# A streaming encoder layer on one Trainium2 core: first level of the triangular inverse by transposes, gate products placed elsewhere in the mixer

## What is computed

```
glu, qkv, b_raw, a_raw, z, gates = jnp.split(xn @ w_in, pts, axis=-1)
c_in = glu[..., :CONV_DIM] * jax.nn.sigmoid(glu[..., CONV_DIM:])
c, conv_new = causal_dwconv(c_in, conv_prev, conv_dw_w)          # 31 taps
c = jax.nn.silu(layer_norm(c + conv_dw_b, conv_ln_g, conv_ln_b))
qkv, dconv_new = causal_dwconv(qkv, dconv_prev, dn_conv_w)       # 4 taps, then silu
...
a_mat = jnp.where(strict, beta[..., :, None] * kk * decay, 0.0) + jnp.eye(chunk)
sol = lax.linalg.triangular_solve(a_mat, rhs, left_side=True, lower=True)
...
delta = u_c - jnp.einsum('bhck,bhkv->bhcv', w_c, s)
o = jnp.einsum('bhck,bhkv->bhcv', qg_c, s) + jnp.einsum('bhij,bhjv->bhiv', qk_c, delta)
s = gl_c[..., None, None] * s + jnp.einsum('bhck,bhcv->bhkv', kd_c, delta)
...
o = o * lax.rsqrt(jnp.mean(o * o, -1, keepdims=True) + EPS) * dn_norm_g
o = o * jax.nn.silu(z)
```

## Time and profile before

| | us |
|---|---|
| three runs | 4794.46, 4795.47, 4798.47 (median 4795.47) |
| span of the profiled execution | 4798.7 |
| projections, 61.6 to 656 | 594.4 |
| layer norm, 656 to 804.4 | 148.4 |
| four prompt tiles, 804.4 to 1375 | 570.6 |
| streams, 1375 to 1566.5 | 191.5 |
| merge, output projection, queries, to 2337 | 770.5 |
| experts, to the end | 2461.7 |

### The profile page before, as it was taken

One profiled execution on the slowest core, in us unless ns is written; L12 is line 12 of the kernel. 1 busy time (PEld: TensorE's weight loads), 2 busy tenths in 40 slices (PEclk: granted clock), 3 DMA queues, 4 the chain that ended last, 5 costly groups with the idle time before them and its releaser, 6 DMA issues. The chain is left out here.

```text
span 4798.7 us, 84568 instructions
## 1 busy us (share of the span) xinstructions
PE 4555.8 (95%) x28205; PEld 4362.4 (91%) x28205; DVE 3410.1 (71%) x4571; ACT 1318.1 (27%) x2054; POOL 1324.8 (28%) x936
## 2 busy tenths in 40 slices
PE   8999989999999999999688999999999999999995
PEld 8999989999998998999678999999999999999994
DVE  4889882334433331068896898888899999999998
ACT  4232323222221221142372222222222222222222
POOL 0111132121212333323002333333333333333333
PEclk8999999999999999999899999999999999999998
DMA  3222323221224433232268999999999999999998
GB/s 119 83 87 87 88 66 98 72 69 60 73 76 154 136 113 144 72 121 70 75 201 330 366 362 365 368 361 367 368 370 381 378 378 375 376 376 374 381 377 332
DMA packets 283687, 1085.62 MB, mean 226 GB/s; under 512 B 23696, under 2 KB 104464, under 8 KB 209936
## 3 DMA queue, kind: packets, MB, share of 16 engines
q0 software_dynamic: 74752, 538.99, 28.6%
q1 hardware_dynamic: 168336, 400.91, 25.3%
q10 hardware_dynamic: 40320, 142.10, 7.6%
HBM read 1017.03 MB, written 64.88 MB: 225 GB/s over the span
## 5 line engine op out<-in xcount | busy, mean ns | idle before, releaser
L489 PE MATMUL ps<-xhi,hi 128*128 128x320 f32 x2560 | 775.4, 316 | 32.2 <-POOL lo L1391 15.6
L489 PE MATMUL ps<-xlo,hi 128*128 128x320 f32 x2560 | 763.7, 311 | 0.0
L2460 PE MATMUL ps<-xhi,whi 128*128 128x384 f32 x2048 | 693.9, 339 | 18.0 <-issue 18.0
L2499 PE MATMUL ps<-ahi,vhi 128*128 128x384 f32 x1536 | 667.5, 435 | 33.8 <-DVE workr L2737 33.8
L2460 PE MATMUL ps<-xlo,whi 128*128 128x384 f32 x2048 | 689.9, 337 | 0.0
L2573 ACT ACTIVATE whi<-work 128x1024 fp32r<-128x1024 f32 x240 | 254.6, 1061 | 1522.3 <-PE ps L2465 1437.3
L2799 DVE CUSTOM_DVE_ANT_0 work<-work,keep 128x2048 f32<-128x2048 f32 x256 | 585.0, 2285 | 35.3 <-DMA work<-in_peer_u,cur_u 23.9
L2764 DVE SCALAR_TENSOR_TENSOR keep<-work,act_w,keep 128x2048 f32<-128x2048 f32 x256 | 600.2, 2345 | 1.9 <-DVE keep L2826 0.9
L2863 POOL DMA_INDIRECT work<-in_peer_v,cur_v x256 | 371.4, 1451 | 754.7 <-DVE keep L2764 729.4
L489 PEld LDWEIGHTS ps<-xhi,hi 128*128 128x128 f32 x2560 | 486.5, 190 | 37.3 <-POOL lo L1391 16.2
L2500 PE MATMUL ps<-alo,vhi 128*128 128x384 f32 x1536 | 520.1, 339 | 0.0
(11 more groups left out here) (336 smaller groups left out, 8186.9 us busy)
## 6 DMA issues: line engine op xcount, KB each, us to landing
work<-in_v_units ACTq DMA_DIRECT2D x256, 512.0 KB, 8.1
work<-in_u_units SPq DMA_DIRECT2D x240, 512.0 KB, 8.0
keep<-in_w_first SPq DMA_DIRECT2D x160, 512.0 KB, 3.6
keep<-in_w_units SPq DMA_DIRECT2D x32, 1024.0 KB, 4.9
gates_dram<-work SPq DMA_DIRECT2D x8, 3072.0 KB, 11.8
gbuf<-gates_dram SPq DMA_DIRECT2D x31, 768.0 KB, 9.6
arena<-in_w_units SPq DMA_DIRECT2D x32, 512.0 KB, 4.0
gates_T<-keep SPq DMA_DIRECT2D x32, 320.0 KB, 2.2
```

The costliest lines, as they stand in the source:

```text
L489: m = pe.matmul(out[:, o:o + HT], w[:, k, :], x[:, 8 * kh + k, c], start=kh == 0 and i == 0, stop=kh == 1 and i == 23)
L2460: pe.matmul(out, h3[:, k, :], (xlo if m % 2 else xhi)[:, 8 * half + k, :], start=half == 0 and m == 0, stop=False)
L2499: pe.matmul(out, vh, a_h, start=False, stop=False)
```

## The change

1. **First level of the inverse.** T starts as the identity, so the first level's products with T are replaced: T's transpose becomes identity minus the masked A (VectorE alone), and T becomes identity minus the transpose of that, which TensorE makes by eight transposes. The identity copies (L1281, L1282), ScalarE's `xc(0)` and the 16 products at L619 and L622 of level 0 go; VectorE writes the mask of level 1 in the same six steps.
2. **Gate filler.** 384 gate matmuls ahead of the layer norm's sums, 228 behind its loop (312 and 300 before). `high` of half 82 moves ahead of the last two spills of q and k on ScalarE, and s and hi steps move among the squares. In a tile 24 follow the new first level (34 in the old), and the tile ends with 58, the output transposes, 30 (before 78, the transposes). In the streams there are 34 ahead of the first head's update, and 72 at the end.
3. **Waits of the projections.** q waits for the sigmoid of the pass before (`evac["gate"]`, whose first count ScalarE gives behind the small chain on `a_log`, L758), and k for `glu_done`.
4. **Streams.** `spread(0)` goes ahead of the output sum, `decay(0)` ahead of the root; the output transposes and last multiply follow head 2.
5. **End.** SP no longer waits for `gate_st` at the end of the mixer; the two places of the next block that need it do.

```diff
-            prompt = {2 * 4: 2 * LEVELS, 2 * 4 - 2: 2 * LEVELS - 2, 2 * 4 + 1: 2 * LEVELS + 1, 4 * 4 - 2: 4 * LEVELS - 2}.get(per, per)
+            prompt = {2 * 4: 2 * LEVELS, 2 * 4 - 2: 2 * LEVELS - 2, 4 * 4 - 6: 4 * LEVELS - 6}.get(per, per)
...
             late_store(7)
             sp.wait_ge(next_ld, 32)
-            sp.wait_ge(gate_st, 16 * 2 * KD)
             sp.wait_ge(out_done, 32)
...
                     if kd == "q":
+                        pe.wait_ge(evac["gate"], c + 1)
+                    elif kd == "k":
                         pe.wait_ge(glu_done, c + 1)
...
-            gates(312)
+            gates(384)
...
-            gates(300)
+            gates(228)
...
                 gates(30)
-                for l in range(lev):
+                w(dd["at"], tot(2, 2))
+                for g in range(2):
+                    w(dd["atl"], tot(2 * lev, g + 1))
+                    for h in range(4 * g, 4 * g + 4):
+                        m = pe.transpose(ps[1][:, h * P:(h + 1) * P], atl[:, h, :], ident)
+                    m.then_inc(dd["x"], 1)
+                gates(24)
+                for l in range(1, lev):
...
-                    gates(78)
+                    gates(58)
+                    out_rows()
+                    gates(30)
                 else:
                     for h in range(H):
-                        gates(32)
+                        gates(34 if h == 0 else 32)
...
+                        if h == 2:
+                            out_rows()
+                    gates(72)
...
             act.sem_inc(norm_root["q"], 1)
+            act.sem_inc(evac["gate"], 1)
...
                 if more:
                     high(c * 10 + 15, 15, wait)
+                else:
+                    high(NPROJ + 2, NPROJ + 2, wait)
                 for kd in "qk":
                     wait(norm_done[kd], c + 2)
                     spill(c, kd)
...
-                    xc(0)
                     s(1, 0)
                     s(1, 1)
                     xc(1)
...
-                lk(v.tensor_copy(tb, bm(ident)))
-                v.tensor_copy(ttb, bm(ident)).then_inc(dd["tt"], 1)
...
+                for g in range(2):
+                    hs = slice(4 * g, 4 * g + 4)
+                    w(dd["atl"], tot(2 * lev, g + 1))
+                    v.tensor_tensor(ttb[:, hs, :], bm(ident, 4), atl[:, hs, :], ALU.subtract).then_inc(dd["tt"], 1)
+                    w(dd["x"], tot(2 * lev, g + 1))
+                    v.tensor_tensor(tb[:, hs, :], bm(ident, 4), ps8(1)[:, hs, :], ALU.subtract).then_inc(dd["t"], 1)
+                    w(dd["tt"], tot(2 * lev, g + 1))
+                    v.tensor_tensor(atl[:, hs, :], atb[:, hs, :], bm(cst[:, LEV0 + 1, :], 4), ALU.mult).then_inc(dd["atl"], 1)
...
             sp.wait_ge(mg_out, 1)
+            sp.wait_ge(gate_st, 16 * 2 * KD)
             gates(1)
...
             merge_weight(1, 1, None)
+            act.wait_ge(gate_st, 16 * 2 * KD)
             split(ohi, of, 3, o_hi)
```

More of the change, by code:

```diff
@@ L291, in build @@
         s1_ld, s2_ld = [sem(f"s1_ld{i}") for i in range(3)], [sem(f"s2_ld{i}") for i in range(5)]
-        gate_mm, gate_act, gate_st = sem("gate_mm"), sem("gate_act"), sem("gate_st")
+        gate_mm, gate_act = sem("gate_mm"), sem("gate_act")
+        gate_st = ctx.enter_context(nc.semaphore("gate_st"))
         gate_out = at(CT + 4096, T)
@@ L406, in _ @@
             next_raw(N0 + 7)
-            sp.wait_ge(dd["tx"], count_s(14, 14))
+            sp.wait_ge(dd["tx"], count_s(10, 10))
             state_1(1)
@@ L541, in gate_steps @@
                 return steps, pos
-            pe.wait_ge(evac["gate"], NC)
+            pe.wait_ge(evac["gate"], NC + 1)
             gates, done = gate_steps(0, NPROJ, NPROJ, lambda s, v: pe.wait_ge(s, v))
-            gates(312)
+            gates(384)
             pe.wait_ge(cconv_out, NC)
@@ L568, in delta, with out_rows @@
                 lev = 4 if streams else LEVELS
+                def out_rows():
+                    w(dd["oscaled"], tot(1, 1))
+                    for h in range(H):
+                        m = pe.transpose(ps[2][:, h * P:(h + 1) * P], xb[:, h, :], ident)
+                    m.then_inc(dd["otr"], 1)
                 gates(0 if streams else 38)
@@ L869, in _ @@
             hi(7)
+            s(3, 0)
+            hi(8)
+            s(3, 1)
+            hi(9)
             for kd in "qkv":
@@ L884, in _ @@
             square(1)
-            s(3, 0)
+            hi(10)
             square(2)
+            s(4, 0)
             square(3)
-            s(3, 1)
-            hi(9)
             square(4)
+            s(4, 1)
+            hi(11)
             square(5)
             square(6)
-            hi(10)
             square(7)
-            s(4, 0)
             act.wait_ge(ln_sqmm, NC)
             act.activation(at(LMEAN, T), ps[2][:, 0:T], ACT.Sqrt, bias=epsc[:, 0:1], scale=1.0 / CONV).then_inc(ln_root, 1)
-            s(4, 1)
-            hi(11)
             hi(12)
+            s(5, 0)
+            s(5, 1)
+            hi(13)
             act.wait_ge(ln_scaled, 1)
@@ L1188, in iteration @@
                 wait(unit_done, c * 10 + 10)
-                wait(evac["gate"], c + 1)
+                wait(evac["gate"], c + 2)
                 wait(prefix_done["c"], c * 16 + 16)
@@ L1323, in delta, with spread, decay, out_rows @@
                 v.tensor_tensor(vc, vc, tb, ALU.subtract).then_inc(dd["r2"], 1)
+                bmask = cst[:, BLK_S, :]
+                def spread(h):
+                    v.tensor_tensor(at(SLOT[3 if h % 2 else 6], NB, P), atl[:, h, :].unsqueeze(1).to_broadcast([P, NB, P]),
+                                    bmask[:, NT - 1::NT].unsqueeze(2).to_broadcast([P, NB, P]), ALU.mult).then_inc(dd["dm"], 1)
+                def decay(h):
+                    st_h = at(S2[h % 5], NB, P)
+                    glb = smalld[:, 64 + NB * h:64 + NB * h + NB].unsqueeze(2).to_broadcast([P, NB, P])
+                    v.wait_ge(s2_ld[h % 5], 16 * (h // 5) + 16)
+                    lk(v.tensor_tensor(st_h, st_h, glb, ALU.mult))
+                def out_rows():
+                    w(dd["otr"], tot(1, 1))
+                    v.scalar_tensor_tensor(oT[:, :, cols], ps8(2), pcol("dn_g"), zT[:, :, cols], ALU.mult, ALU.mult).then_inc(dd["out"], 1)
                 w(dd["ks"], tot(2, 2))
                 lk(v.tensor_tensor(xb, ps8(2), bc(smalld[:, 32:40]), ALU.mult))
+                w(dd["r2"], tot(1, 1))
+                if streams:
+                    w(dd["dlc"], tot(1, 1))
+                    spread(0)
                 w(dd["o2"], tot(1, 1))
                 lk(v.tensor_tensor(xb, xb, ps8(1), ALU.add))
-                w(dd["r2"], tot(1, 1))
                 lk(v.tensor_tensor(eb, xb, xb, ALU.mult))
@@ L1334, in delta @@
                 v.sem_inc(dd["oss"], 1)
+                if streams:
+                    decay(0)
                 w(dd["oroot"], tot(1, 1))
@@ L1372, in _ @@
             with v.Fori(0, PT) as t:
-                NLK = 18
+                NLK = 17
                 lk = Link(v, "dve", dd_link_d, base=t * NLK, loop=True)
```

64 lines of the change are left out of this document (22 added, 42 removed).

## The result

The changed kernel takes 4835.8 us (median of 4 runs, 4833.3 to 4848.8), the kernel before 4796.1 beside it: a ratio of 1.0081 with a 95% interval of 1.0062 to 1.0099. It is slower by 40 us, where 31 us less were forecast. The profiled execution has a span of 4831.7 us, 33.0 more than the one of before.

What follows compares the result with a forecast made beforehand. TensorE was taken to bound layer norm and tiles, though not alone, and the ScalarE and VectorE chain the projections. Terms of +7.0, -3.2, -2.7, -11.5, -7.8, -7.2, -5.0 and -1.0 sum to -31.4: 4795.5 to 4764 us, range 4757 to 4787.

Steps and rivals of the forecast that it cites:

- Later stages are not changed: Stages behind the mixer, the expert loops among them: assumed to keep their time, so no term in the sum.
- the low-clock windows of later loops: Loops behind the changed code: low-clock windows may fall otherwise by a few us when all before them is shifted.
- the one for a slower result: Tile ends: so much more half-rate clock that the gain is used up; 4806 us at 21 us more each, chance 0.03.
- Start +7.0: First projection pass: q waits for its new semaphore, given behind L758, so the first product comes 7.0 us later.
- Passes -3.2: Later projection passes: q starts 3.2 us earlier, a lead that counts once, in the last pass; the period stays.
- Layer norm -2.7: Layer norm: a 5.5 us wait and low clock go, a 3.8 us wait for `s(0,0)` comes; net -2.7 us.
- Held low part -11.5: Layer norm: TensorE's 10.1 us wait for GpSimd's long low part of half 84 and its low clock go, -11.5 us.
- Tiles: Level 0's products go, new waits of 0.7 and 2.3 us come: -7.8 us for three tiles, -7.2 at the fourth's end.
- The gap behind the branch: Tile loop's branch: its 2.5 us gap stays but for -0.2 us, since a branch's cost is its own.
- Streams -5.0: Streams: first level cheaper by 4.4 us, a wait of 4.3 us left at head 1, other small terms; net -5.0 us.
- end -1.0: Mixer's end: transposes, last multiply and SP's wait go, but all engines still meet before the next block; -1.0 us.
- its third: Layer norm: the term for GpSimd's held low part, whose wait and low clock were to go, -11.5 us.

## Why the prediction was wrong

The step that failed is a sentence at the end of the sum: "Later stages are not changed". Their source isn't, and their instructions come in the same order, but 80 matmuls with their weight loads and some register steps fewer ahead of them moved both expert loops by 182 instructions against loads of 256. That brought the second loop from a place where it ran without a load (none on queue 8 from 3870 to 4540 us) to one where it is loaded again in every pass (43 packets there; a gap of 2.0 to 3.0 us five times, with low clock behind four), and the first from a bad place to a worse one (a second gap of 4.0 to 5.0 us, six times). The term was put at nothing and measured 61.6 us, more than twice the 28.7 that the mixer gained. The prediction did allow the low-clock windows of later loops "a few us"; it had no waits there, and no rival had this mechanism; the one for a slower result, low clock at the tile ends, didn't occur: one tile end of four had 3.4 us of it. The trace of before had the row that spoke: six gaps of 3 us at the first loop's pass ends and none in the second, in loops of the same length.

Point by point, for the mixer:

- **Start +7.0**: the wait was 7.1 to 9.4 us in seven profiles, and undone it gave back 6.2. **Passes -3.2**: the period stayed at 74.4 to 74.5, the last pass took 68.6 instead of 71.8. Both sizes were right; only the row that the passes would wait in was another, as said above.
- **Layer norm -2.7**: the wait for `s(0,0)` was 4.5 instead of 3.8, and low clock stood behind it for 3.4 or 6.8 us. Missed was the load queue: a step that moves 72 products ahead of the sums delays the layer norm's output, on which SyncE's `conv_dram` store, three row loads and the next half weight wait in a row: 4.2 us, and half of 3.4 or 6.8 us of low clock. In profiles without the hold the first tile's first own product (L574) came at 799.9 before and at 806 to 807 now, +6 where 7.0 - 3.2 - 2.7 = +1.1 was summed.
- **Held low part -11.5**: 14 to 15 us in the two profiles compared, but by chance: before's mixer has it in three of five. As a mean it is worth more like (3/5 - 1/9) x 14.5 = 7.
- **Tiles**: predicted waits of 2.3 and 0.7 measured 2.2 and 0.6; a tile without low clock takes 139.4 to 140.0 us against 140.9 to 141.7, and fewer have it. The gap behind the branch, 2.1 to 2.5 before and left at that but for 0.2, came to 1.2 to 1.7; that a branch's cost is its own was the author's estimate, and no run shows it. From first tile to streams the means over the profiles are 552.8 against 565.3 us: -12.5, where 15.0 were summed.
- **Streams -5.0, end -1.0**: the wait was 4.0 instead of 4.3, and idle time at the merge 7.1 instead of 8.1; together 186.6 against 195.7 us as means, -9.1, more than summed; which part of it was mis-sized wasn't taken apart.

Without the hold, the mixer gained 13 us: the merge came at 1557.7 and 1560.6 before, and at 1545.4 to 1547.2 with the change in four profiles. The prediction's terms without its third give 19.9. That the two profiles compared first show 28.7, near the 31.4 of the sum, is luck.

Like with like, with both engines' loops in the same places, the change takes 4762.6 us against 4783.0 for the kernel before, 20 us; by the ratios to the kernel before that ran beside each it is 16, and the two intervals overlap, so the size is rough. Behind the merge the changed kernel is the slower one even so: 3205 to 3211 us in seven profiles against 3199.2 in the one of before. TensorE waits longer there for VectorE's `workr`, 22.6 to 28.5 us against 16.2 (2600 to 4760 us). What of this is one fast execution, and what the shifted starts cost, is open; timing is out as the cause of the 61.6 us, not of these 6 to 12.

## What to carry to other kernels

A change in one stage can move the code of all later ones: here by 182 TensorE instructions, at 61.6 us behind the mixer. Before forecasting that untouched stages keep their time, look for waits for "issue" at the ends of loop passes and for the queues of kind "instruction" beside them; where a hot loop is near the length of these, 1664 instructions or 6.5 of TensorE's loads, time the change with a few idle instructions ahead of that loop, at more than one place, before it is judged. And a stall seen in one profile is one draw: ask for a second before it goes into a sum.

## What the runs showed of the hardware

- The granted TensorE clock was 1.00 or 0.50 in every record of the 14 profiles.
- TensorE's code came in packets of 16 KB, 255.9 and 257.2 recorded instructions apart in two stretches without a branch back. On queue 14 the packets were of 8 KB, and when VectorE's code alone was moved by 101 instructions they went from four to three at a pass end, and VectorE's gaps of 3.1 us went. A TensorE loop of 1664 instructions ran for 850 us without a load when it touched seven such blocks by the count of 256; the head of a loop that was never loaded again stood at five different places (40, 57, 73, 103 and 120 instructions behind a border, which is worked out from the place of the second gap).
- At eight touched blocks a pass cost nothing, one gap of 1.9 to 3.6 us, or two of 1.7 to 3.1 and 3.9 to 5.5 us, each most often with 3.4 to 10.2 us of low clock behind it. The same kernel had six such passes of six in one profile and four of six in another.
- Idle instructions alone made the kernel before 0.9990 (193 of them) or 1.0099 (74) of its time; with VectorE's code moved too it went down to 0.9957.
- A GpSimd subtraction that took 2.4 to 2.9 us for the halves around it took 15.9 us beside VectorE's taps (18.8 for two in a row), in some executions of a mixer and not in others.
